# The second feed-forward of a two-block network: blocks multiplied with seven products in place of eight

## The reference, cut to what matters

```
def swiglu(h, w_in, w_out):
    g, u = jnp.split(h @ w_in, 2, axis=-1)
    return (jax.nn.silu(g) * u) @ w_out
...
        h = rms_norm_2(x, norm_g[l, 2]) * (1.0 + sc2) + sh2
        x = x + g2 * rms_norm_2(swiglu(h, ffn_w_in[l], ffn_w_out[l]), norm_g[l, 3])
```

## Time and profile before

| | |
|---|---|
| median of 3 runs | 2539.11 us (2537.85 to 2542.91) |
| the profiled execution, span | 2541.9 us |
| PE busy | 2358.2 us, 93% of the span |
| POOL busy | 1071.4 us, 42% |
| DVE busy | 1319.0 us, 52% |
| ACT busy | 857.2 us, 34% |
| the last feed-forward on PE | 2165.2 to 2531.5 us, 366.3 us, 1584 matmuls |

### The profile page before, as it was taken

The page is one execution under the profiler, slowest core; times in us unless marked ns, Lnnn a source line. Parts: engine busy times, 40 slices in busy tenths (PEclk is TensorE's granted clock), DMA queues, the critical chain, the costliest instruction groups (busy, mean ns, idle before and its releaser), DMA issues.

```text
span 2541.9 us, 34272 instructions
## 1 busy us (share of the span) xinstructions
PE 2358.2 (93%) x13550; PEld 1981.7 (78%) x13550; DVE 1319.0 (52%) x2032; ACT 857.2 (34%) x1649; POOL 1071.4 (42%) x800
## 2 busy tenths in 40 slices
PE   5998899988989889889999999999898999999998
PEld 4787787777878656679989989898786667788886
DVE  6885737966559664473533424234587765111013
ACT  2124242124232666634221212113313873322222
POOL 3343445324363332325542434334552443645544
PEclk9999999989989999999999999999999999999999
DMA  8550125510224200021322313232441004223332
GB/s 282 176 172 1 35 67 169 159 55 1 90 81 123 55 2 1 9 92 51 125 75 83 108 56 119 84 91 83 131 155 33 1 2 133 91 91 100 94 98 75
DMA packets 148759, 219.00 MB, mean 86 GB/s; under 512 B 18484, under 2 KB 73172, under 8 KB 148472
## 3 DMA queue, kind: packets, MB, share of 16 engines
q1 hardware_dynamic: 148600, 216.82, 27.1%
HBM read 214.69 MB, written 2.10 MB: 85 GB/s over the span
## 4 chain that ended last, share of the span: by engine, by line
PE 56%; DVE 4%; ACT 3%; POOL 2%; issue 2%; DMA 1%; ACTq 0%; DVEq 0%; POOLq 0%; SPq 0%
PE ps L307 14%; PE ps L309 14%; PE ps L308 14%; PE ps L1094 5%; PE ps L1122 3%; PE ps L1144 2%; PE ps L1391 1%; PE ps L1141 1%; DVE mod_acc_aux L367 1%; POOL h_transposed L580 1%; PE ps L1386 1%; PE ps L394 1%; PE ps L592 1%; POOL w_lo L296 0%; ACT att_probs_two L1184 0%
## 5 line engine op out<-in xcount | busy, mean ns | idle before, releaser
L296 POOL TENSOR_TENSOR w_lo<-w_raw,w_hi 128x1024 fp32r<-128x1024 f32 (+3 forms) x252 | 593.2, 2355 | 1000.6 <-ACT w_hi L289 1000.5
L289 ACT ACTIVATE w_hi<-w_raw 128x1024 fp32r<-128x1024 f32 (+3 forms) x252 | 255.7, 1016 | 1158.1 <-PE ps L309 957.5
L307 PE MATMUL ps<-w_hi,h_transposed 128*128 128x512 f32 (+3 forms) x1136 | 428.5, 377 | 58.1 <-POOL w_lo L296 30.9
L308 PE MATMUL ps<-w_lo,h_transposed 128*128 128x512 f32 (+3 forms) x1136 | 418.8, 369 | 0.0
L309 PE MATMUL ps<-w_hi,h_transposed 128*128 128x512 f32 (+3 forms) x1136 | 418.6, 369 | 0.0
L307 PE MATMUL ps<-h_transposed,w_hi 128*128 128x384 f32 (+1 forms) x1056 | 372.8, 353 | 5.0 <-POOL h_transposed L580 3.3
L309 PE MATMUL ps<-h_transposed,w_lo 128*128 128x384 f32 (+1 forms) x1056 | 372.2, 352 | 0.0
L308 PE MATMUL ps<-h_transposed,w_hi 128*128 128x384 f32 (+1 forms) x1056 | 372.1, 352 | 0.0
L307 PEld LDWEIGHTS ps<-w_hi,h_transposed 128*128 128x128 f32 x1136 | 224.0, 197 | 100.7 <-POOL w_lo L296 36.6
L367 DVE SCALAR_TENSOR_TENSOR mod_acc_aux<-w_raw,c_act,mod_acc_aux 128x512 f32<-128x512 f32 x266 | 263.7, 1013 | 47.3 <-DMA w_raw<-in_w_mod_dram 22.0
L308 PEld LDWEIGHTS ps<-w_lo,h_transposed 128*128 128x128 f32 x1136 | 224.0, 197 | 32.6 <-issue 2.2
(11 more groups left out here) (323 smaller groups left out, 3532.6 us busy)
## 6 DMA issues: line engine op xcount, KB each, us to landing
w_raw<-in_ada_w_dram SPq DMA_DIRECT2D x96, 512.0 KB, 4.0
w_raw<-in_ffn_w_in_dram SPq DMA_DIRECT2D x88, 512.0 KB, 3.6
w_raw<-in_w_mod_dram SPq DMA_DIRECT2D x48, 512.0 KB, 4.7
w_raw<-in_ffn_w_out_dram SPq DMA_DIRECT2D x44, 512.0 KB, 3.7
w_raw<-in_w_in_dram SPq DMA_DIRECT2D x40, 512.0 KB, 4.3
w_raw<-in_w_out_dram SPq DMA_DIRECT2D x16, 512.0 KB, 4.1
w_raw<-in_od_w_in_dram SPq DMA_DIRECT2D x16, 512.0 KB, 3.8
mod_gain<-in_norm_g_dram SPq DMA_DIRECT2D x16, 256.0 KB, 4.6
```

Of the source, the lines that this page charges most:

```text
L289: act.activation(w_hi[:, i % 2, 0:k * n], w_raw[:, u % 4, 0:k * n], ACT.Copy).then_inc(w_hi_ready.sem, 1)
L296: pool.tensor_tensor(w_lo[:, i % 2, 0:k * n], w_raw[:, u % 4, 0:k * n], w_hi[:, i % 2, 0:k * n].bitcast(F32), ALU.subtract).then_inc(w_lo_ ...
L307: pe.matmul(acc, left[0], right[0], start=start, stop=False)
L308: pe.matmul(acc, left[0], right[1], start=False, stop=False)
```

## The change

A new phase, `FeedForwardBySeven`, takes the place of the last `FeedForward`. Group 0 is multiplied as before. For groups 1 to 10, and for the output products of groups 0 to 9 in pairs, both operands are cut into two by two blocks (for `w_in`: 256 tokens by 512 of the contraction, and 512 of the contraction by the 256 up or gate columns; for `w_out`: 256 tokens by 256 of the contraction, and that by 512 columns). The two by two product is then made with seven block products in place of eight, with sums and differences of blocks as operands and of results (Winograd's form of Strassen's scheme). One stage is the seven units of one group's `w_in` or of one pair's `w_out`. The order of stages is in 1, out of pair 0, then in 2p, in 2p+1, out of pair p for p = 1 to 4, then in 10. The output product of group 10 ends the phase as before. In the prediction an odd stage is an in stage of an odd group, an even stage that of an even group.

The seven units of a stage are named by the left operand, in the order of `ROW`. On PE an in unit is 24 matmuls of 256 columns, an out unit 12 matmuls of 512 columns. Four of the seven right operands come from memory (as many loads as before). The other three, and the one that is made in place in `w_raw`, are differences that DVE makes from SBUF to SBUF, 128 x 1024 each (`difference`, four per stage). ACT and POOL split all seven. `w_hi` and `w_lo` get a third place each, so ACT may write unit i once PE has finished unit i-3.

The split of the hidden values moves from POOL to DVE (`part_lows`). The left blocks of h and their sums are made by DVE at the start. The results of block products are added by DVE between PE's units, and PE waits for these steps, since a bank holds a running sum that is read between two units.

```
+                for p in range(self.pairs):
+                    self.stages += [("in", 2 * p)] if p else []
+                    self.stages += [("in", 2 * p + 1), ("out", p)]
+                self.stages.append(("in", GROUPS - 1))
...
+                    u11 = ring_slot(sp, (w_lo_ready, i0 + 1), (t_made, t + 1))
...
+                    u21 = ring_slot(sp, (w_lo_ready, i0 + 2), (t_made, t + 4))
...
+                    u12 = ring_slot(sp, (w_lo_ready, i0 + 5))
...
+                    u22 = ring_slot(sp, (w_lo_ready, i0 + 6))
...
+                    splits.append((raw(u11), *landed(u11)))
+                    splits.append((raw(u21), *landed(u21)))
+                    splits.append((made_second[:, :], t_made, t + 2))
+                    splits.append((made_first[:, :], t_made, t + 1))
+                    splits.append((raw(u12), t_made, t + 3))
+                    splits.append((raw(u22), *landed(u22)))
+                    splits.append((made_second[:, :], t_made, t + 4))
...
+                if which == 1:
+                    dve.wait_ge(at11.sem, n11)
+                    dve.wait_ge(at12.sem, n12)
+                    if k:
+                        dve.wait_ge(w_lo_ready.sem, self.unit[k - 1] + 4)
+                    ins = dve.tensor_tensor(made_first[:, :], b12, b11, ALU.subtract)
+                if which == 2:
+                    dve.wait_ge(at22.sem, n22)
+                    if k:
+                        dve.wait_ge(w_lo_ready.sem, self.unit[k - 1] + 7)
+                    dve.wait_ge(t_made.sem, t + 1)
+                    ins = dve.tensor_tensor(made_second[:, :], b22, made_first[:, :], ALU.subtract)
+                if which == 3:
+                    ins = dve.tensor_tensor(b12, b22, b12, ALU.subtract)
+                if which == 4:
+                    dve.wait_ge(at21.sem, n21)
+                    dve.wait_ge(w_lo_ready.sem, i0 + 3)
+                    ins = dve.tensor_tensor(made_second[:, :], b21, made_second[:, :], ALU.subtract)
+                ins.then_inc(t_made.sem, 1)
...
+                        for q in range(7):
+                            act.wait_ge(w_used.sem, i + q + 1)
+                            self.high_at(act, i + q + 3)
+                            if q == 0:
+                                self.part(act, p, "s4", sums_at[1][:, 2], mid + 7)
+                                self.part(act, p, "a22", sums_at[1][:, 1], mid + 4)
+                        continue
...
+                        self.part(act, p, "a12", up, mid + 3)
+                        self.high_at(act, i + 9)
+                        self.part(act, p, "s2", sums_at[0][:, 0], mid + 6)
+                        self.part(act, p, "s1", sums_at[0][:, 1], mid + 5)
...
+            def part_lows(self, dve, count, name, src):
+                dve.wait_ge(part_high.sem, count)
+                z = sevens[name]
+                dve.tensor_tensor(z[:, 1], src, z[:, 0].bitcast(F32), ALU.subtract).then_inc(part_low.sem, 1)
...
+                f = lambda a, b: h_kept[:, 4 * a:4 * a + 4, 256 * b:256 * b + 256]
+                dve.wait_ge(ht_low.sem, src.g0 + len(src.groups))
...
+                self.difference(dve, 0, 1)
+                for i, (name, z) in enumerate((("s1", f(1, 1)), ("s2", f(0, 0)), ("s3", f(0, 1)))):
+                    dve.wait_ge(rows_high.sem, self.rh0 + i + 1)
+                    r = self.rows(name)
+                    dve.tensor_tensor(r[:, 1], z, r[:, 0].bitcast(F32), ALU.subtract).then_inc(rows_low.sem, 1)
+                self.difference(dve, 0, 2)
+                self.difference(dve, 0, 3)
...
+                dve.tensor_tensor(first[:, 2], first[:, 0], first[:, 1], ALU.subtract).then_inc(part_made.sem, 2)
+                dve.wait_ge(rows_high.sem, self.rh0 + 4)
+                r = self.rows("s4")
+                dve.tensor_tensor(r[:, 1], f(1, 0), r[:, 0].bitcast(F32), ALU.subtract).then_inc(rows_low.sem, 1)
+                self.part_lows(dve, self.ph0 + 1, "a11", first[:, 0])
+                self.part_lows(dve, self.ph0 + 2, "s3", first[:, 2])
...
+                    dve.wait_ge(sums_kept.sem, self.copied[k] + 1)
+                    dve.wait_ge(w_used.sem, i + 2)
+                    dve.tensor_tensor(up, up, c_sums, ALU.add).then_inc(sums_left.sem, 1)
+                    self.difference(dve, k, 4)
+                    dve.wait_ge(sums_kept.sem, self.copied[k] + 3)
+                    dve.wait_ge(w_used.sem, i + 5)
+                    dve.tensor_tensor(gate_two, gate_two, a_sums, ALU.add).then_inc(sums_left.sem, 1)
+                    self.difference(dve, k + 1, 1)
+                    dve.wait_ge(w_used.sem, i + 6)
+                    dve.tensor_tensor(gate_one, gate_one, c_sums, ALU.add).then_inc(sums_left.sem, 1)
+                    self.difference(dve, k + 1, 2)
+                    dve.wait_ge(gated_silu.sem, self.silu_of[k] + 2)
+                    dve.tensor_tensor(up, up, gate_one, ALU.mult).then_inc(part_made.sem, 1)
...
+                    else:
+                        one, two = sums_at[0][:, 0], sums_at[0][:, 1]
+                        dve.wait_ge(sums_left.sem, left + 4)
+                        dve.tensor_tensor(two, two, gate_two, ALU.add).then_inc(part_made.sem, 2)
+                        self.part_lows(dve, ph + 3, "a12", up)
+                        dve.wait_ge(part_made.sem, mid + 5)
+                        dve.tensor_tensor(one, two, one, ALU.subtract).then_inc(part_made.sem, 1)
+                        dve.wait_ge(part_made.sem, mid + 6)
+                        dve.tensor_tensor(gate_one, up, one, ALU.subtract).then_inc(part_made.sem, 1)
+                        self.difference(dve, k + 1, 3)
+                        self.part_lows(dve, ph + 4, "s2", one)
+                        self.part_lows(dve, ph + 5, "s1", two)
+                        self.part_lows(dve, ph + 6, "s4", gate_one)
+                        self.part_lows(dve, ph + 7, "a22", gate_two)
...
+                for q, (bank, half, n) in enumerate(((a_bank, 0, 0), (c_bank, 0, 0), (a_bank, 0, 1), (c_bank, 1, 1), (a_bank, 1, 1), (c_bank, 0, 1),
+                                                     (a_bank, 1, 0))):
+                    y = Y[:, 2 * half:2 * half + 2, n * HALF:(n + 1) * HALF]
+                    dve.wait_ge(w_used.sem, i + q + 1)
+                    if q in (1, 4, 5):
+                        dve.wait_ge(sums_left.sem, left + {1: 1, 4: 4, 5: 3}[q])
+                    if p == 0 and q in (0, 2, 3, 6):
+                        ins = dve.tensor_copy(y, ps[:, bank:bank + 2, :])
+                    else:
+                        ins = dve.tensor_tensor(y, y, ps[:, bank:bank + 2, :], ALU.add)
+                    ins.then_inc(sums_left.sem, 1)
+                    if q == 1:
+                        self.difference(dve, k, 4)
+                    if q in (4, 5, 6):
+                        self.difference(dve, k + 1, q - 3)
...
+                        if q in (0, 1):
+                            if k == 1:
+                                self.wait(pe, f_silu, 1)
+                                self.wait(pe, f_full, 2)
+                            elif k > 1:
+                                pe.wait_ge(sums_left.sem, self.left[k - 2] + ((4, 3) if self.stages[k - 2][0] == "in" else (7, 6))[q])
+                        elif kind == "in":
+                            sig, n = ((sums_kept, kept + 1), (sums_left, left + 1), (sums_kept, kept + 2), (sums_kept, kept + 3),
+                                      (sums_left, left + 2))[q - 2]
+                            pe.wait_ge(sig.sem, n)
+                        else:
+                            pe.wait_ge(sums_left.sem, left + q - 1)
+                        bank = c_bank if q % 2 else a_bank
...
+                            pe.wait_ge(part_low.sem, self.l0 + 7 * g + (1, 3, 4, 5, 5, 6, 7)[q])
+                            z = sevens[name]
...
-            schedule.append(NormTransposed(False, 6, 7, (4, GROUP)))
-            schedule.append(FeedForward(a["ffn_w_in_2"][1], a["ffn_w_out_2"][1], XT))
+            schedule.append(NormTransposed(False, 6, 7, (4, GROUP), h_kept))
+            schedule.append(FeedForwardBySeven(a["ffn_w_in_2"][1], a["ffn_w_out_2"][1]))
```

More of the change, by code:

```diff
@@ L228, in build @@
         act_t = take("ffn_hidden", [P, 2, 6, TOK], F32R)
+        Y_END = arena + XT * D * 4
+        w_hi3, w_lo3 = at("w_hi_third", [P, 1024], F32R, Y_END), at("w_lo_third", [P, 1024], F32R, Y_END + D * 4)
+        made_first = at("block_difference", [P, 1024], F32, gate_rows_at)
+        made_second = at("block_second_difference", [P, 1024], F32, gate_rows_at + D * 4)
+        sevens = {name: at("ffn_" + name, [P, 2, 2, 2 * P], F32R, arena + (XT + CT) * D * 4 + i * 4096)
+                  for i, name in enumerate(("a11", "s3", "a12", "s2", "s1", "s4", "a22"))}
+        h_kept = at("h_kept", [P, KT, S], F32, arena + 41984)
+        row_s3 = at("row_s3", [P, 2, KT // 2, 2 * P], F32R, XT * D * 4)
```

(26 more changed lines are left out.)

308 lines of the change are left out of this document (287 added, 21 removed).

## The result

The kernel after takes 2603.22 us (median of 4 runs, 2595.26 to 2609.3), the kernel before 2538.48 beside it (2532.74 to 2542.91): 1.0251 times the time, 95% interval 1.0227 to 1.0275, slower by 2.5%. Predicted were 2593 and a range of 2526 to 2618.

The account below looks back on a forecast made before the run. PE was taken to bound the last feed-forward. Terms of -30 + 3.5 + 7 + 9 + 55 + 10 gave +54.5 us, a median of 2593 us; range 2526 to 2618 (8 times in 10), own range 2575 to 2618.

Parts of the forecast that it names:

- PE's own work: Last feed-forward: seven block products at 0.12 us per 256 columns take less matmul time on PE, -30 us.
- The boundary: Odd stage to its out stage: PE's third unit waits for DVE's first output sum, 11 us five times, +55.
- the walk: Step-by-step timing of queued operations at stage boundaries, with DVE and POOL taking turns; out-stage stall 12.9 us as upper end.
- Stages in between: Odd stages behind even ones wait 1.7 us each, even stages 0.5 each: +9 us (0 to 25).
- Start: Phase start: DVE's work on the left blocks meets about five turns with POOL, +7 us (0 to 9).
- End: Group 10's output products wait for that group's product, rounding and low part alone, +3.5 us.
- The clock: PE runs at half clock after each of five boundary waits, 2 us each: +10 us (0 to 13).
- no exclusion: Rival: DVE's and POOL's turns mostly miss each other, boundaries cost 3.1 us each: 2528 us, chance 0.13.
- Half the turns: Rival: POOL runs out of free places and leaves DVE alone, boundary 6 us: 2554 us, chance 0.24.
- Whole length: Rival: a DVE operation holds POOL off for all its length, boundary 15 us: 2635 us, chance 0.08.

Follow-up runs that it names:

- narrow_both: Kernel after, with POOL's low parts cut to 8 of 1024 columns and five of DVE's to 8 of 512 from pair 1 on: 2523.57 us, ratio 0.9942.
- narrow_pool: Kernel after, with POOL making only 8 of 1024 columns of each low part in the units by seven: 2533.47 us, ratio 0.9971.
- keep_short: Kernel after, with 18 matmuls on constants on PE ahead of the third unit of each out stage: 2599.06 us, ratio 1.0216.
- narrow_parts: Kernel after, with DVE's low parts of a12, s2, s1, s4 and a22 cut to 8 of 512 columns from pair 1 on: 2580.8 us, ratio 1.0185.
- by_need: Kernel after, with DVE's and ACT's work around the out stages reordered by what PE needs next: 2591.4 us, ratio 1.0202.
- edges: Kernel after, with work reordered at the start, from even to odd stages and at the end: 2608.81 us, ratio 1.026.
- shared_lows: Kernel after, reordered around the out stages, with DVE making the first three of each out stage's seven low parts instead of POOL: 2569.28 us, ratio 1.0107.

## Why the prediction was right, and where a term was not

The mechanism held and most sizes did, against 2603 for a forecast of 2593. In the phase +54.5 us were forecast and +64.8 came. Two readings below need the clock. Here is a stretch of pair 1 at the half clock, as a row by stretch, and the starts of the second and third unit around it:

```profile
2294.21:2297.62 3.41, 3.39 (x9) 2.08 (x7) 3.38 (x4) 1.85 (x3) 0.98 (x1) 0.50 0.00 0
```

```profile
2293.09 0.47 PE L335 MATMUL ps<-w_hi,ffn_a 128*128 128x512 f32 x1 [2.48 <-DVE ffn_a L1946]
2305.54 0.77 PE L335 MATMUL ps<-w_hi_third,ffn_s 128*128 128x512 f32 x1 [7.94 <-DVE y_tokens L2077]
```

Term by term:

- *PE's own work*, -30: measured -27.3 in narrow_both, and about -31.5 without the 4.2 that the half clock cost there. The distance of 0.12 us for 256 columns held.
- *The boundary*, +55 (15 to 65): the waits are 44.1 before the third units and 12.3 for a12, 56.4. In every pair the third unit began 12.4 to 12.5 us behind the second. So where the second unit ran at the half clock (pairs 1 and 3), its longer run only filled the wait: 7.9 in place of 9.4. Without that the boundaries cost some 60, 12 each. I had taken 11, less than the walk's 12.9 because a turn might fall away. Behind a12 none did. narrow_pool shows that the turns with POOL are the cause, since the rest of DVE's queue alone leaves 2.64.
- *Stages in between*, +9: 5.9 behind ACT's copy and 3.1 of small waits for POOL, 9.0. That the sum agrees is luck in part. Each odd stage behind an even one lost 2.0, of it 1.5 before the third unit, where the walk had 0.5, and the even stages 0.2 at most. ACT's copy was late because it stands in ACT's queue behind s3, whose sum (L2016) had met a turn.
- *Start*, +7: 5.2, with four whole turns in place of five (operations of 1.21 us that took 3.33 to 3.43). *End*, +3.5: 3.4.
- *The clock*, +10 (0 to 13): this term was mis-sized. The matmuls that ran at 0.50 fill 37.5 us of the phase, in nine stretches, half of it, 18.7, lost. Behind the third units 24.2 us ran so, which is 12 lost by this count and 11 by keep_short. Behind a12's waits of pairs 1 and 3 it was 3.4 us each, which cost no time, as said above: in keep_short all five second units met the half clock, and their third units still began 12.4 to 12.5 us behind them. The start's wait had 3.6 us behind it and the end's 2.9, 3.2 lost, which I had not counted. So the clock cost about 15.

The terms as measured are -31.5 + 60 + 9 + 5.2 + 3.4 + 15 = 61. No run shows the 4 that are missing to 64.8. An estimate: the last matmul before a wait counts with its whole length, 0.39 us, where the next one would have started 0.23 behind it, and the kernel after has 19 waits more than narrow_both, which makes 3. The forecast was 10 us low: the boundary and the clock are 5 of it each and these 4 come on top, while PE's own work and the start came 3 cheaper.

Of the rivals, "no exclusion" (2528) describes what narrow_pool made by leaving out POOL's work: 2533, with 2.64 at each boundary where the rival had 3.1. "Half the turns" named a true mechanism, that POOL runs dry and lets DVE pass, and narrow_parts shows it at work; in the kernel after it did not act at the boundaries, where all five have the same three turns. "Whole length" fell: POOL's low part took 3.43 us at most behind a difference of 1.22, which is 1.0 over its 2.40, and 2.78 to 2.84 behind one of 0.69, which is 0.4. The Trainium skill (SBUF — State Buffer, Who interferes with whom) has the lock held for the whole operation; this case's traces, before and after, show less, by 0.2 to 0.3 us.

What stays open: whether a better division of the low parts between DVE and POOL would bring the change below 2538. The three tries moved waits more often than they removed them. narrow_both, with nearly all of those low parts left out, gained 14 us with the order of the kernel after; what another order would gain on top of it was not tried.

## What to carry to other kernels

A change that saves an engine's arithmetic by more elementwise work must be costed by what that work meets. Here 27 us of saved matmuls stood against 96 us of DVE's time spent behind POOL, and a sum built on a walk through one boundary in the order of the queue, with the durations that the trace shows for two engines at work together, gave +54 us where +65 came (the whole time to 0.4%). Look for work from SBUF to SBUF that is new on DVE while POOL is busy, and count turns, not microseconds. And when a fix only changes the order, list the waits again unit by unit: a new order alone (by_need, edges) brought 12 us at most and moved waits to other units, and the 34 us of shared_lows came with work taken off POOL.

## What the runs showed of the hardware

- DVE and POOL with all inputs in SBUF took turns: a DVE operation that found POOL busy ended 0.55 us (512 columns) or 1.08 us (1024 columns) behind POOL's end, and operations of 0.15 us passed four at a time once POOL had nothing ready. DVE operations with an input in PSUM were not held: 1.22 for each sum into `y_tokens` in the boundary, beside POOL or not.
- Waits of PE of 2.5 us were followed by 3.4 us at the half clock in two of the five pairs, while those of 2.2 and 2.6 in the other three were not. Around each of those of 7.9 to 9.4 stood 10.2 us at the half clock, which began within the wait and held 3.0 to 6.1 us of matmuls. The half clock of the second units cost nothing, since they were followed by a wait for DVE: from the second to the third unit it was 12.4 to 12.5 us in every pair.
- A float32 matmul of 256 columns on constants took 0.432 us, in two records 0.216 apart, 3.6 times the 0.12 of the fp32r matmuls of that width.
